# A second set of third expert matrices copied by GpSimd, and router logits from scaled rows with the shift as one added row

## What is computed

```python
grp_logits = t @ w_grp + b_grp                  # 4 columns
exp_logits = t @ w_exp + b_exp                  # 32 columns
g_sel = top_k(grp_logits, 1); top_val, top_idx = top_k(exp_logits[g_sel], 2)
top_w = softmax(top_val) * softmax(grp_logits)[g_sel]
for each expert e:
    hid = silu(t @ w1[e]) * (t @ w3[e])         # 1024 -> 256
    out += gate[e] * (hid @ w2[e])              # 256 -> 1024
```

## Time and profile before

| | us |
|---|---|
| median of 3 runs (1205.75 to 1207.89) | 1206.84 |
| profiled execution, its own time | 1208.46 |
| its span, first to last instruction | 1206.7 |
| PE busy in the span | 1113.0 (92%) |
| PEld busy | 925.3 (77%) |
| DVE busy | 729.5 (60%) |
| ACT busy | 504.6 (42%) |
| POOL busy | 107.9 (9%) |
| mean granted clock of TensorE | 0.973 of 2.4 GHz |

### The profile page before, as it was taken

One profiled execution on the slowest core, in us unless ns is written; L12 is line 12 of the kernel. 1 busy time (PEld: TensorE's weight loads), 2 busy tenths in 40 slices (PEclk: granted clock), 3 DMA queues, 4 the chain that ended last, 5 costly groups with the idle time before them and its releaser, 6 DMA issues. The chain is left out here.

```text
span 1206.7 us, 18909 instructions
## 1 busy us (share of the span) xinstructions
PE 1113.0 (92%) x7709; PEld 925.3 (77%) x7710; DVE 729.5 (60%) x1084; ACT 504.6 (42%) x850; POOL 107.9 (9%) x123
## 2 busy tenths in 40 slices
PE   7998899999899999999998999999999899797666
PEld 5896699999789978999987878988787666464333
DVE  4577777777866667777877537655456543323223
ACT  4557443443455545344345434445544322222111
POOL 5000001001000000001100000000000022222220
PEclk9999999999999999999999999999999799898888
DMA  9952377787654244878764453645665749989995
GB/s 274 296 174 78 128 240 278 270 302 276 215 190 160 106 140 140 319 276 295 276 237 122 88 174 105 199 156 182 203 216 200 313 192 370 417 364 413 422 422 217
DMA packets 120740, 285.02 MB, mean 236 GB/s; under 512 B 11581, under 2 KB 72250, under 8 KB 108000
## 3 DMA queue, kind: packets, MB, share of 16 engines
q1 hardware_dynamic: 110608, 248.77, 57.5%
q0 software_dynamic: 10064, 35.32, 8.9%
HBM read 281.87 MB, written 2.20 MB: 235 GB/s over the span
## 5 line engine op out<-in xcount | busy, mean ns | idle before, releaser
L1862 DVE TENSOR_TENSOR w_lo<-ring,w_hi 128x1024 fp32r<-128x1024 f32 (+1 forms) x272 | 319.4, 1210 | 93.9 <-ACT w_hi L1409 84.8
L1409 ACT ACTIVATE w_hi<-ring 128x1024 fp32r<-128x1024 f32 (+1 forms) x272 | 277.7, 1050 | 154.8 <-PE acc L648 130.9
L646 PE MATMUL pp<-x_hi,w_hi 128*128 128x256 f32 x896 | 257.4, 287 | 5.0 <-DVE w_lo L1862 2.9
L647 PE MATMUL pp<-x_lo,w_hi 128*128 128x256 f32 x896 | 253.4, 283 | 0.0
L648 PE MATMUL pp<-x_hi,w_lo 128*128 128x256 f32 x896 | 253.4, 283 | 0.0
L646 PEld LDWEIGHTS pp<-x_hi,w_hi 128*128 128x128 f32 x896 | 171.6, 191 | 12.4 <-issue 7.3
L647 PEld LDWEIGHTS pp<-x_lo,w_hi 128*128 128x128 f32 x896 | 171.7, 192 | 1.4 <-issue 0.2
L648 PEld LDWEIGHTS pp<-x_hi,w_lo 128*128 128x128 f32 x896 | 171.6, 191 | 0.0
L646 PE MATMUL acc<-w_hi,x_hi 128*128 128x512 f32 (+2 forms) x320 | 127.2, 397 | 5.3 <-DVE x_lo L1847 4.1
L648 PE MATMUL acc<-w_hi,x_lo 128*128 128x512 f32 (+2 forms) x320 | 122.9, 384 | 0.0
L647 PE MATMUL acc<-w_lo,x_hi 128*128 128x512 f32 (+2 forms) x320 | 122.8, 384 | 0.0
(11 more groups left out here) (361 smaller groups left out, 1764.3 us busy)
## 6 DMA issues: line engine op xcount, KB each, us to landing
ring<-in_w_up_dram SPq DMA_DIRECT2D x32, 1024.0 KB, 5.4
ring<-in_w_down_dram SPq DMA_DIRECT2D x32, 1024.0 KB, 6.5
exp_ring<-in_w_dram SPq DMA_DIRECT2D x32, 1024.0 KB, 17.5
stage<-in_w_ada_dram POOLq DMA_DIRECT2D x48, 512.0 KB, 6.3
ring<-in_w_in_dram SPq DMA_DIRECT2D x24, 1024.0 KB, 5.4
big<-in_w_dram SPq DMA_DIRECT2D x24, 1024.0 KB, 14.8
mod<-in_w_dram SPq DMA_DIRECT2D x16, 1024.0 KB, 15.3
ring<-in_w_in_a_dram SPq DMA_DIRECT2D x12, 1024.0 KB, 14.9
```

The source lines that it names most:

```text
L646: pe.matmul(out, lhs[0], rhs[0], start=start, stop=False)
L647: pe.matmul(out, lhs[0], rhs[1], start=False, stop=False)
L1409: act.activation(shaped(high_half(b, k), raw), raw, ACT.Copy).then_inc(S["hi_ready"], 1)
L1862: dve.tensor_tensor(shaped(low_half(b, k), raw), raw, shaped(high_half(b, k), raw), ALU.subtract).then_inc(S["lo_ready"], 1)
```

## The change

- **w3 gets a second set**, `w3_next`, in buffers that are free by then: `q_t`, `h_tm`, `rows`, and half of one in `mod`, the other half in a new buffer. SyncE loads w3(s+1) there; GpSimd copies it into `w3_slots` when it has landed and `w3_used` allows, behind its copies of w1, and counts `w3_moved`, for which TensorE's up1 waits.
- **w3(1) is loaded ahead of the loop**, at the places where its four buffers come free: after `lg_ready`, `tables_done` (new) and `res_in` (new, after `residual_in(1)`).
- **SyncE's loop** becomes w1(s+1), w2(s), w3(s+1), and each matrix of w1 and w3 waits for the copy of its own predecessor.
- The load of `rows_b` (the final norm's row, 512 KB over all partitions) moves from the middle of the kernel behind GpSimd's last copy. `passed` moves from `q_t` to `mod`.
- **The router's logits** are made of the scaled rows alone, turned as soon as `scale` has written them (`m_ready`). The shift's part is the same for all tokens: TensorE turns the shift row into 8 columns (`shift_columns`), multiplies them by `w_rt` and adds the bias (`shift_row`, 9 matmuls), and spreads the row over 128 partitions (`every_row`). ScalarE copies each of these out. VectorE makes logits = product * rstd + that row, in four instructions instead of three copies.
- `shift` writes the reordered rows to `u_tm` itself, so ScalarE's `router_rows` goes. Three filler matmuls (`busy`) are added on TensorE, two behind `residual_in(0)`, one ahead of the first gather. The tables of quads and limits are made ahead of the first residual.

The diff, cut to its core:

```diff
+        w3_next = [(q_t[:, :, :].rearrange("p a b -> p (a b)"),), (h_tm[:, :, :].rearrange("p a b -> p (a b)"),),
+                   (rows[:, :, :].rearrange("p a b -> p (a b)"),), (mod[:, 4096:5120], w3_half[:, :])]
...
             sp.wait_ge(S["u_done"], QT)
+            sp.wait_ge(S["lg_ready"], 1)
             load_w2(0, 3)
             load_w2(0, 2)
+            load_w3(1, 0)
+            load_w3(1, 2)
+            sp.wait_ge(S["tables_done"], 1)
+            load_w3(1, 3)
+            sp.wait_ge(S["res_in"], 1)
+            load_w3(1, 1)
...
                 done = sp.value_load(tabs[0:1, s - 1:s], min_val=1, max_val=CHUNKS)
-                sp.wait_ge(S["w3_used"], done)
-                for e in range(4):
-                    load_w3(s, e)
+                if s + 1 < QUADS:
+                    for e in range(4):
+                        sp.wait_ge(S["w1_moved"], 4 * (s - 1) + e + 2)
+                        load_w1(s + 1, e)
                 sp.wait_ge(S["w2_used"], done)
                 for e in range(4):
                     load_w2(s, e)
                 if s + 1 < QUADS:
-                    sp.wait_ge(S["w1_moved"], 4 * s + 1)
                     for e in range(4):
-                        load_w1(s + 1, e)
+                        sp.wait_ge(S["w3_moved"], 4 * (s - 1) + e + 2)
+                        load_w3(s + 1, e)
...
                     pool.tensor_copy(w1_slots[:, e, :], w1_slots[:, 4 + e, :]).then_inc(S["w1_moved"], 1)
+                pool.wait_ge(w3_here[0], 16 * s)
+                pool.wait_ge(S["w3_used"], done)
+                for e in range(4):
+                    parts = w3_next[e]
+                    width = 2048 // len(parts)
+                    if e:
+                        pool.wait_ge(w3_here[e], 16 * len(parts) * s)
+                    for k, part in enumerate(parts):
+                        moved = pool.tensor_copy(w3_slots[e][:, width * k:width * k + width], part)
+                        if k + 1 < len(parts):
+                            link(moved)
+                    moved.then_inc(S["w3_moved"], 1)
+            pool.wait_ge(S["w3_moved"], 4 * (QUADS - 1) + 1)
+            pool.dma_start(rows_b, bass.AP(A["final_norm_2"].tensor, 0, [[0, 128], [1, 1024]]))\
+                .then_inc(S["rowsb_in"], 16)
...
-                pe.wait_ge(S["u_ready"], q + 1)
+                pe.wait_ge(S["m_ready"], q + 1)
                 tile_to_feature_major(o_tm, q)
...
+            def shift_columns():
+
+                for k in range(KT):
+                    last = pe.matmul(acc[:, 0, k:k + 1], mod[0:1, 3072 + 128 * k:3200 + 128 * k],
+                                     con("ones", 1)[:, 0:1], start=True, stop=True)
+                last.then_inc(S["cols_mm"], 1)
+
+            def shift_row():
+
+                pe.wait_ge(S["cols_done"], 1)
+                for k in range(KT):
+                    pe.matmul(acc[0:1, 1, 0:36], modc[:, 0, k:k + 1], w_rt[:, k, :], start=(k == 0), stop=False)
+                pe.matmul(acc[0:1, 1, 0:36], con("ones", 1)[:, 0:1], brow[0:1, 0:36], start=False, stop=True)\
+                    .then_inc(S["crow_mm"], 1)
+
+            def every_row():
+
+                pe.wait_ge(S["crow_done"], 1)
+                pe.matmul(pp[:, 0, 64:100], con("ones", 1), brow[0:1, 0:36], start=True, stop=True)\
+                    .then_inc(S["crow_mm"], 1)
...
-            for q in range(QT):
-                last = logits(q, turn_rows(q))
-            last.then_inc(S["lg_ready"], 1)
+            tile0 = turn_rows(0)
+            shift_columns()
+            logits(0, tile0)
+            tile1 = turn_rows(1)
+            shift_row()
+            logits(1, tile1, every_row).then_inc(S["lg_ready"], 1)
             residual_in(0)
+            busy(2, tp[:, 0, :])
...
+            busy(1, tp[:, 0, :])
             pe.wait_ge(S["u_done"], QT)
             pe.wait_ge(S["sel_ready"], 1)
             gather(0)
             gather(1)
-            residual_in(1)
+            residual_in(1).then_inc(S["res_in"], 1)
...
-                pe.wait_ge(S["w3_full"], quad * 64 + 64)
+                pe.wait_ge(S["w3_full"], 64)
+                pe.wait_ge(S["w3_moved"], quad * 4 + 1)
                 up(1, lambda e, cols: w3_slots[e][:, cols]).then_inc(S["w3_used"], 1)
...
             router_turned(0)
+            act.wait_ge(S["cols_mm"], 1)
+            act.activation(modc[:, 0, :], acc[:, 0, 0:8], ACT.Copy).then_inc(S["cols_done"], 1)
             router_squares(1)
             router_root(1)
-            router_rows(0)
             router_turned(1)
-            router_rows(1)
+            act.wait_ge(S["crow_mm"], 1)
+            act.activation(brow[0:1, 0:36], acc[0:1, 1, 0:36], ACT.Copy).then_inc(S["crow_done"], 1)
+            act.wait_ge(S["crow_mm"], 2)
+            act.activation(lg_shift, pp[:, 0, 64:100], ACT.Copy).then_inc(S["crow_done"], 1)
...
-                link(dve.tensor_tensor(o_tm[:, q, :], h_tm[:, q, :], mod[:, 4096:5120], ALU.mult))
+                dve.tensor_tensor(o_tm[:, q, :], h_tm[:, q, :], mod[:, 4096:5120], ALU.mult).then_inc(S["m_ready"], 1)
...
-                dve.scalar_tensor_tensor(o_tm[:, q, :], o_tm[:, q, :], rstd[:, q:q + 1], mod[:, 3072:4096],
-                                         ALU.mult, ALU.add).then_inc(S["u_ready"], 1)
+                dve.scalar_tensor_tensor(u_tm[:, q, :].rearrange(by_tile, k=KT), o_tm[:, q, :].rearrange(by_row, k=KT),
+                                         rstd[:, q:q + 1], mod[:, 3072:4096].rearrange(by_row, k=KT),
+                                         ALU.mult, ALU.add).then_inc(S["u_done"], 1)
...
             dve.wait_ge(S["lg_ready"], 1)
+            dve.wait_ge(S["crow_done"], 2)
             for q in range(QT):
-                dve.tensor_copy(lg_groups[:, q, :], pp[:, q, 0:4])
-            link(dve.tensor_copy(lg_experts[:, :, :].rearrange("p (q g) e -> p q (g e)", q=QT), pp[:, :, 4:36]))
+                dve.scalar_tensor_tensor(lg_groups[:, q, :], pp[:, q, 0:4], rstd[:, q:q + 1], lg_shift[:, 0:4],
+                                         ALU.mult, ALU.add)
+                last = dve.scalar_tensor_tensor(lg_experts[:, 4 * q:4 * q + 4, :].rearrange("p g e -> p (g e)"),
+                                                pp[:, q, 4:36], rstd[:, q:q + 1], lg_shift[:, 4:36], ALU.mult, ALU.add)
+            link(last)
```

More of the change, by code:

```diff
@@ L140, in program @@
         hid_hi = sb("hid_hi", [128, 2, 2, SEQ], f32r)
+        with nc.sbuf_tensor("w3_rest", [128, 1024], f32) as w3_rest:
+            w3_half = w3_rest
         hid_lo = sb("hid_lo", [128, 2, 2, SEQ], f32r)
@@ L250, in program @@
         warm = sb("warm", [128, 1])
+        spare = sb("spare", [128, 1])
         squares = scr[:, 0, 0:1024]
@@ L294, in program @@
         w1_here = [sem(f"w1_here{e}") for e in range(4)]
+        w3_here = [sem(f"w3_here{e}") for e in range(4)]
         ada_full = [sem(f"ada_full{i}") for i in range(2)]
@@ L434, in load_w3 @@
             def load_w3(s, e):
-                load_part(w3_slots[e], w3[4 * s + e, :, :, :], S["w3_full"])
+                if s == 0:
+                    load_part(w3_slots[e], w3[e, :, :, :], S["w3_full"])
+                    return
+                parts = w3_next[e]
+                n = KT // len(parts)
+                for k, part in enumerate(parts):
+                    load_part(part, w3[4 * s + e, :, n * k:n * k + n, :], w3_here[e])
             def load_w2(s, e):
@@ L562, in _ @@
                 .then_inc(S["rowsg_in"], 16)
-            pool.dma_start(rows_b, bass.AP(A["final_norm_2"].tensor, 0, [[0, 128], [1, 1024]]))\
-                .then_inc(S["rowsb_in"], 16)
             pool.dma_start(w_rt[:, :, 0:4], A["w_grp_2"][0, :, :].rearrange("(k p) n -> p k n", p=128))\
@@ L1224, in turn_rows, with logits @@
             def turn_rows(q):
-                pe.wait_ge(S["u_ready"], q + 1)
+                pe.wait_ge(S["m_ready"], q + 1)
                 tile_to_feature_major(o_tm, q)
                 return groups[0]
-            def logits(q, turned_at):
+            def logits(q, turned_at, between=lambda: None):
                 for kt in range(KT):
@@ L1234, in logits @@
                         emptied(turned_at - 2 + kt // 4)
-                    pe.matmul(pp[:, q, 0:36], q_t[:, kt, q * 128:(q + 1) * 128], w_rt[:, kt, :],
-                              start=(kt == 0), stop=False)
-                return pe.matmul(pp[:, q, 0:36], con("ones", 1), brow[0:1, 0:36], start=False, stop=True)
+                    if kt == 4:
+                        between()
+                    last = pe.matmul(pp[:, q, 0:36], q_t[:, kt, q * 128:(q + 1) * 128], w_rt[:, kt, :],
+                                     start=(kt == 0), stop=(kt == KT - 1))
@@ new lines, in logits @@
+                return last
+            def shift_columns():
[9 more added lines that the diff above has]
+                    .then_inc(S["crow_mm"], 1)
@@ L1239, in residual_in @@
+            def every_row():
```

(21 more changed lines are left out.)

30 lines of the change are left out of this document (17 added, 13 removed).

## The result

| | median us (runs) | ratio to before, 95% interval | profiled execution | its span |
|---|---|---|---|---|
| before | 1208.19 (7) | | 1208.46 | 1206.7 |
| after | 1199.72 (7) | 0.993 (0.9909 to 0.995) | 1199.16 | 1197.3 |

The change makes the kernel 0.7% faster, 8.5 us by the medians. The forecast was 6.0 us less; the forecast range held the time. But two of its parts were off in opposite directions, and the rest of this text is about them.

The account below looks back on a forecast made before the run. The prediction took the expert stage to be bound by its weight transfers, with holes. Expert stage -5.1 and router -0.9 sum to -6.0 us: a span of 1200.7 for 1206.7, median 1200.8; forecast 1198 to 1204.4, wider range 1194 to 1208.

Parts of the forecast that it names:

- two of its parts: Expert stage with the second w3 set: 5.1 us won; router, up to the first round's start: 0.9 us won.
- the clock falling at about 949.2 as before: Router, first tile's logits: TensorE's clock drops to half there, so these eight matmuls take 2.6 us, ending at 950.5.
- warm TensorE: Rival, chance 0.12: full clock through router and final up1; first round 6.4 us earlier, up1 2.3 less, total 1193.0.
- So the stalls are filled with the added matmuls and nothing is won: Router on TensorE: added matmuls take up the old waits; logits end at 957.9 instead of 957.43, +0.4 us.
- w2(1) at u+30: First round: w2(1) lands 30 us after that round's start, as before, its load waiting for w2's use at 16.7 us.
- the tail: Last quad: w3(7) landed 199.1 us after the first round's start, copy 2.2, up1 5.9, then 6.1 to the w2 matmuls.
- the slower rival: Chance 0.08: GpSimd's copies shut VectorE out, second-round selections of quads 1 and 3 come 11.4 us late each, total 1223.6.
- Both holes of the second rounds: Transfers behind the second rounds of quads 1 and 3: holes of about 2 us stay, w1's wait replacing w3's.

Follow-up runs that it names:

- after's fourth: The changed kernel without an edit, a further profiled execution: 21.0 us from the output product's end to the first round, 230.5 from there to the end.
- last w3 direct: The changed kernel, but the last quad's w3 is loaded straight into the slots TensorE reads and not copied: ratio to before 0.9926.
- selection first: The changed kernel, but GpSimd starts its copies of w1(1) only when VectorE's first-round selection is written: ratio to before 0.9915.
- the third profile: The changed kernel without an edit, one more execution: 24.2 us from the output product's end to the first round, 229.5 from there to the end.
- second set of runs: The changed kernel without an edit, measured again beside later variants: ratio to before 0.9932.
- the w3 set alone: The changed kernel with the router's old form and no fillers, keeping the second w3 set and its queue order: ratio to before 0.9978.
- the stall put back: The changed kernel with one added wait: TensorE's first router turn waits for the second tile's residual: ratio to before 0.999.

## Why the prediction was right in sum and wrong in its parts

- **The clock in the router: the term that was mis-sized.** The step was "the clock falling at about 949.2 as before", and from it half clock to the fillers' end: 27.2 from R to u. Measured 21.2, 24.2, 24.2 and 21.0. Counted from R, the clock fell 4.5 and 2.1 us behind it in before's two profiles, with the stall, and 9.1, 5.5 and 5.1 in three of after's, without it; in after's fourth, in "last w3 direct" and in the second profile of "selection first" it did not fall at all between 949 and 965 (granted 1.00). I had weighed the clock on the narrow matmuls alone. Putting 2.05 us of stall back cost 0.6% and lowered the mean granted clock of the executions from 0.976 and 0.974 to 0.9695: what stood before these matmuls counts as well. The "warm TensorE" rival, held at 0.12, came true in the router in two of four profiles (21.2 and 21.0 from R to u, its own figure is 21.7), and half in the other two.
- **The warm rival's total did not come true.** After's fourth profile had full clock in the router and in the last up1, and its span was 1197.1, not 1193.0. From u to the end it took 230.5, where the rival's terms give 226.6. So the forecast of the expert stage was too low by 3.9 us even with a warm TensorE.
- **The case nearest to the forecast** is the third profile, where the clock fell 5.1 behind R (4.5 in the forecast). There the sum can be set against its rows. The logits end at R+11.5, forecast R+13.2: the first tile's logits were still at full clock (1.97 for 2.6), and the second turn was for two thirds (1.51 for 1.97). From there to the position matmuls 5.3 for 6.1: the clock came back 3.9 us into the dense work, I took 5. The rest 7.5 for 7.9. The shift row was 1.25 for 1.3. The sizes at half clock were right; the moments at which the clock turned were not.
- **"So the stalls are filled with the added matmuls and nothing is won"** was the wrong reading. Filling a stall wins nothing in time when counted by itself, but here it kept TensorE at full clock longer.
- **The first round.** w2(1) at u+30 was forecast with the first round's w2 matmuls ending at u+16.7, as before, and from a queue that is empty at u. With u 6 us earlier VectorE's selection met GpSimd's copies, these matmuls ended at u+17.7, and the queue had run full until about then; w2(1) landed at u+31.6. The sum counted VectorE's wait for copies only in the second rounds. In the third profile, with u at R+24.2, it was u+30.6.
- **Quad 3 and the tail, in after's first profile.** The last w3 was forecast at u+199.1 and landed at u+202.5. Of the 3.4: w2(3) lands 1.0 later (95.7 for 94.7), its w2 matmuls 2.3 (6.01 for 3.7: TensorE has stood 5.26 us ahead of them, and the clock is at 0.50; a cold w2 was in no term of the sum. The second set makes w3 early and so gathers the quad's idle time in front of w2), the second round 1.0 less (16.5 for 17.5), the 32 MB behind it 84.3 for 83.2. Then the copies 2.5 for 2.2, up1 5.35 for 5.9, to the w2 matmuls 6.0 for 6.1: u+216.4. The expert stage thus won 2.2 for 5.1. In the third profile it won 4.5: there the landing was 0.7 nearer to u and up1 took 3.7.
- **Right as forecast:** no request waits for `w3_used` itself; the end hangs on GpSimd's copy and the last up1 (at half clock in the first profile, at full clock in the third and fourth) and no more on w2(7), which has been there since about 1177; the columns cost 2.0 (1.94); VectorE gets in between two copies, 1.79 and 1.90 us, so the slower rival did not occur. Both holes of the second rounds stay, 2.4 and 4.4 us in after; I had 2.4 and about 4.
- **In sum:** R to the end 256.0 forecast; 253.0, 256.6, 253.7 and 251.5 measured. That -6.0 stands so near to the medians' -8.5 and (second set of runs) -6.7 is partly luck, two errors that cancel: too little for the router, too much for the experts.

What stays open: why the clock falls at another moment in each execution of the same kernel, and why R varies. On the first, the Trainium skill ("TensorE: Matmul & The Clock Gate", Part 1: The HAM clock gate) says that the hardware judges TensorE's activity on a schedule that runs freely and does not start with the kernel. By that rule two executions with the same instructions can fall at different moments, as the 9.1, 5.5 and 5.1 us here did; no run here tests it.

## What to carry to other kernels

A short stall ahead of narrow matmuls can cost more than its own length if the clock falls behind it; price its removal from executions with and without it, and not from the row of the stall. When a start mark moves, ask what does not move with it: here VectorE's selection and the fill of the transfer queue, and each took back part of the gain. A prefetch that brings one matrix early gathers the idle time in front of the next one, and what runs behind it can be at half clock. A staging copy is paid at the last use; that loading the last set directly pays (1.2 to 3.6 us by the profiles) is likely and not shown by the medians.

## What the runs showed of the hardware

- TensorE's granted clock differs between executions of the same instructions: over 949 to 953 and 953 to 957 us it was 1.00 and 0.57, 0.95 and 0.50, and 0.50 and 0.50 in three profiles of after, in each of which TensorE had no idle time there.
- With about 2 us of idle ahead of the first turn the first tile's logits took 2.48, 3.62, 3.63 and 3.63 us (before twice, the w3 set alone, the stall put back); without it they took 1.97 or 1.98 in all twelve profiles. In "stall put back" they start at R+5.2, behind the fall, and in after at R+2.8, so a part of that difference is their place. Over all executions the mean granted clock is 0.9695 with the stall put back (median of 12) and 0.976 and 0.974 without it (7 and 6 of after).
- 32 matmuls of w2 took 6.01, 4.91 and 5.34 us in after where TensorE had stood 5.26, 6.35 and 6.23 us ahead of them (quad 3's first round, quads 5 and 6), and 3.64 where it had stood 0.75 or less.
- 64 matmuls of the last up1 took 3.66 and 3.67 us behind 3.28 and 3.39 us of idle, and 5.35 behind 3.59, 3.65 and 3.75 (after's profiles, the second of "selection first", the w3 set alone).
- From 946 to 1004 us one core's DMA engines moved 408 GB/s in after, with one dip to 238 from 983 to 986; over 990 to 997 it was 425.
